# Order of the four products of a quarter tile: both 512-column ones, then both 256-column ones

## The chip, the cores and the metric

The kernel runs on one core of a Trainium2 chip, in one launch. The metric is the device time of that core in microseconds, the median of the runs. Every number below is for this single core.

## The reference, cut to what matters

Two transformer-like blocks run over 256 tokens of width 2048, all in float32. What costs time is the product of the activations with about 400 MB of weights, each weight used once:

```python
# first block: adaptive norm, a wide input projection, a chunked RWKV-7 state, a short convolution
proj = (rms_norm(x, pre_gain) * (1 + scale) + shift) @ w_in     # 2048 x 12416
m = sigmoid(g_a) * ((y_a * silu(z_a)) @ p_a) + sigmoid(g_b) * ((y_b * silu(z_b)) @ p_b)
x = x + gate * rms_norm(m @ w_out, post_gain)                   # 2048 x 2048
# second block: sparse attention (compressed, selected, window), feed-forward, last gate
h = h + nsa_mixer(rms_norm_2(h), ...)                           # w_in 2048 x 5168, w_out 2048 x 2048
h = h + square(relu(rms_norm_2(h) @ ffn_w1)) @ ffn_w2           # 2048 x 8192, 8192 x 2048
h = h + (p @ ple_w_proj) * sigmoid(rms_norm_2(h) @ ple_w_gate)  # 2048 x 2048
```

## The kernel before, in words

**One tile of weights.** Weights come from HBM as a stream of tiles, 128 partitions x 1024 float32 (512 KB), into a ring `raw` of 8. ScalarE copies each tile to `whi` in the type float32r, which TensorE takes in one pass (line 737), VectorE writes the rounding error `raw - whi` to `wlo` (line 1319), both into a ring `wsp` of 4 (`SPLIT`). Activations stand as 512 columns: 256 tokens rounded (the "high" half) and their 256 rounding errors (the "low" half).

**The products.** Weights are the stationary operand, activations the moving one. For one 128 x 128 block of weights TensorE issues two products: `whi` times all 512 columns (line 2197), and `wlo` times the first 256 columns (line 2198). Both accumulate in one PSUM bank; a later step adds the two halves of the bank. Each product is a weight load (LDWEIGHTS) and a matmul, and nothing is shared between two products. A 128 x 1024 tile holds two row blocks `k` (0, 1) by four output blocks `n` (0 to 3). The two row blocks of one `n` are a quarter tile: four products, 512, 256, 512, 256 columns, all into bank `n`. Its last product signals `quarters`, by which ScalarE knows that ring space is free and when a bank is complete.

**`use` (line 2186)** does one tile, or with `part` half of one. In front of a tile it waits for `raw_used` (VectorE has finished the split of this tile, so `whi` and `wlo` are both there), and at the first tile of an output block it waits for `evac_done` (the bank has been read out). `block_of` is eight tiles, the whole depth of 2048. All stages share one TensorE stream written out by hand:

- the opened tiles (`opened_tile`, lines 2246 to 2248), which use three 256-column products per block, then the rest of the first projections (`REST`);
- the `slot(h)` stage: the rest of the input projection, half tiles with the short products of the RWKV-7 chain (`both`, line 2317) between them;
- both output projections of the first block (line 2571, not through `use`), then its `w_out` (tiles `WO0`), the projections of the sparse attention (`NS0`, `QUERY`, `KV0`), its gate columns (lines 2617 and 2618: the same two products with 64 columns of weights) and a compression (line 2632);
- the attention's remaining projections (`NG0`) with attention work between half tiles, then its output projection (`out_tile`);
- the feed-forward part (`ffn`) and the last gate (`PG0`; its last block is three 256-column products, lines 2813 to 2815).

Of the kernel before, what the change touches and what calls it, by code (L numbers as in the profile page):

```python
# [8 lines left out]
P = 128  # L9
T = 256  # L10
D = 2048
KT = D // P
# [276 lines left out]
def block_of_two_layers(nc, stream, vec_in, con_in, x_in, ple_in, lora_in, cmp2_in, out):  # L289
    ctx = ExitStack()  # L290
    with ctx:
# [1891 lines left out]
        def _(pe):  # L2183
            mm = nc.tensor.matmul

            def use(g, i=0, per=RAW, act=None, kt=0, last=KT - 1, bank=0, part=(0, 1, 2, 3), evac=None, off=0):


                n0 = g - WA0
                if part[0] == 0:  # L2190
                    pe.wait_ge(raw_used, i * per + (RAW + in_stream(g) + 1))
                for n in part:
                    if kt == 0 and evac is not None:
                        pe.wait_ge(evac_done, evac[0] + (evac[1] + n + 1))
                    for k in range(2):
                        c = k * 512 + n * P
                        mm(ps[bank + n][:, :], whi[:, n0 % SPLIT, c:c + P], act[:, off + kt + k, :], start=kt + k == 0, stop=False)  # L2197
                        ins = mm(ps[bank + n][:, 0:T], wlo[:, n0 % SPLIT, c:c + P], act[:, off + kt + k, 0:T], start=False,  # L2198
                                 stop=kt + k == last)
                    ins.then_inc(quarters, 1)  # L2200

            def block_of(g0, i, act, evac, per=RAW):

                for j in range(8):
                    use(g0 + j, i, per, act, 2 * j, evac=evac)

            def square_sum(use_, sq_a, sq_t=None, tiles=0):

# [84 lines left out]
            w = OPENED  # L2293
            for r, (blk_, first) in enumerate(REST):
                for j in range(first, 8):
                    use(WA0 + w, act=acts, kt=2 * (j - first), last=KT - 1 - 2 * first, off=2 * first,
                        evac=None if r == 0 else (4 * EARLY + 4 * r - 4, 0))
                    w += 1
            pe.wait_ge(evac_done, 4 * EARLY)
# [8 lines left out]
                        ins.then_inc(quarters, 1)  # L2308
            pe.wait_ge(s.con_loaded, 32)
            def slot(h):  # L2310
                use(WB0 + h // 2, 0, RAW, acts, h // 2 * 2 % KT, part=(0, 1) if h % 2 == 0 else (2, 3),
                    evac=((29 if h >= 16 else 28), h // 16 * 4))

            def both(dst, stationary, moving, start=True, stop=True):
# [259 lines left out]
            E += 32  # L2574
            for j in range(8):
                pe.wait_ge(s.m_done, 2 * j + 2)
                use(WO0 + j, act=acts, kt=2 * j, evac=(E - 4, 0))
            with pe.Fori(1, 4) as b:
                block_of(WO0, b, acts, (b * 4, E - 4))
            E += 16  # L2580
            pe.wait_ge(s.pes_lo, 1)
            for b in range(4):
# [18 lines left out]
            pe.wait_ge(s.pr_out, 6)  # L2601
            for j in range(8):
                pe.wait_ge(s.acts_ready, KT + 2 * j + 2)
                use(NS0 + j, act=acts, kt=2 * j, evac=(E - 4, 0))
                for c in range(2 * j, 2 * j + 2):
                    pe.wait_ge(s.tile_sq, 4 + c + 1)
                    ins = mm(ps[4][:, 0:T], ones, sqx[:, c, :], start=c == 0, stop=c == KT - 1)
            ins.then_inc(s.ss_ps, 1)
            for j in range(8):
                use(NS0 + 8 + j, act=acts, kt=2 * j, evac=(E, 0))  # L2610

            n0 = (GT0 - WA0) % SPLIT
            pe.wait_ge(raw_used, RAW + in_stream(GT0) + 1)
# [27 lines left out]
            for n, kind in enumerate(MIXED):  # L2641
                m = MIXED[:n].count(kind)
                if kind == "C":
                    compress(m)
                else:
                    use(QUERY[m], act=acts, kt=2 * m, evac=(E + 4, 0))
                if n == 8:
                    folded(0)
                if n == 4:
                    pe.wait_ge(s.gt_sig, 1)  # L2650
                    for q in range(2):
                        ins = nc.tensor.transpose(ps[5][:, q * GCOL:(q + 1) * GCOL], gsum[:, q * P:(q + 1) * P], ident[0:GCOL, 0:GCOL])
                    ins.then_inc(s.gt_ps, 1)
            for j in range(8):
                use(KV0 + j, act=acts, kt=2 * j, evac=(E + 8, 0))
                if j == 1:
                    folded(1)
                if j == 5:
                    pe.wait_ge(s.cmp2_in, 16)
                    pe.wait_ge(s.blk_done, 4)  # L2660
                    pe.wait_ge(s.gt_done, 2)
                    mm(ps[4][:, 0:NB], cmp2[:, 0:P], hid[:, 0, :], start=True, stop=True).then_inc(s.cmp_ps, 1)
                    pe.wait_ge(s.hrep_done, GQ)
                    for g in range(GQ):
                        ins = mm(four(5)[:, g, :], hrep[:, g, :], cmp2[:, P:2 * P], start=True, stop=True)
                    ins.then_inc(s.cmp_ps, 1)
# [91 lines left out]

            for g in range(3):
                for k in range(32):  # L2760
                    use(NG0 + 16 * g + k // 2, act=acts, kt=k // 2 * 2 % KT, part=(0, 1) if k % 2 == 0 else (2, 3),
                        evac=(E + 4 * (4 + 2 * g + k // 16) - 4, 0))
                    attention(g, k)
            E += 4 * NG

            def out_tile(j, kt, first, last, e):
                for x in range(2):
                    use(NO0 + j, act=hidn, kt=kt - first, last=last - first, part=(0, 1) if x == 0 else (2, 3), evac=(e - 4, 0),
                        off=first)
                    if j < 12:  # L2770
                        attention(3, 2 * j + x)
# [65 lines left out]
```

## Time and profile before

| | |
|---|---|
| median of 3 runs | 2188.1 us (2186.29 to 2188.31) |
| profiled execution, its own time | 2201.99 us |
| its span, first to last instruction | 2200.3 us |
| TensorE matmul busy | 2163.2 us, 98% |
| TensorE weight loads busy | 1865.9 us, 85% |
| VectorE, ScalarE, GpSimd busy | 71%, 50%, 5% |
| mean DMA rate over the span | 193 GB/s |

The profile gives each matmul a start and a duration, and the durations of neighbours overlap, since matmuls are pipelined. So busy time says little of pace; the distance between two starts does. "Slot" below is the distance from the start of one matmul to the start of the next, "512 slot" that of a 512-column matmul. "PE" is TensorE's matmuls, "PEld" its weight loads, "DVE" VectorE, "ACT" ScalarE.

### The profile page before, as it was taken

How to read it: one execution, taken by the hardware profiler on the slowest of the kernel's cores; microseconds unless marked ns; L12 is line 12 of the kernel's file. 1: busy time of each engine (PE TensorE's matmuls, PEld its weight loads, DVE VectorE, ACT ScalarE, POOL GpSimd, SP SyncE). 2: the span in 40 equal slices, each digit the busy share in tenths (PEclk: the TensorE clock that was granted, in tenths of full speed). 3: DMA queues.
4: the chain of work that ended last, by engine and by line, in shares of the span. 5: the costliest groups of instructions: out<-in, count | busy, mean ns of one | idle time of the engine just before them, and what ended most of it. 6: DMA issues, size and time to landing. Idle time of an engine off the chain costs nothing.

```text
span 2200.3 us, 39494 instructions
## 1 busy us (share of the span) xinstructions
PE 2163.2 (98%) x14640; PEld 1865.9 (85%) x14640; DVE 1571.9 (71%) x2382; ACT 1106.0 (50%) x1749; POOL 109.2 (5%) x96
## 2 busy tenths in 40 slices
PE   8999999999999999999999999999999999999997
PEld 6998887888888888888888878888888888888887
DVE  6985887888887687678666667665575566567767
ACT  3444554555554565465544455444454454445454
POOL 0000000000000100200000002000000000000203
PEclk9999999999999999999999999999999999999999
DMA  9995455455555576566434445556556555555552
GB/s 362 406 377 185 163 182 173 154 173 173 182 164 182 188 252 218 198 199 216 163 126 134 144 153 173 189 183 191 186 167 205 177 192 179 192 189 177 183 181 90
DMA packets 116284, 424.76 MB, mean 193 GB/s; under 512 B 13232, under 2 KB 13616, under 8 KB 115904
## 3 DMA queue, kind: packets, MB, share of 16 engines
q1 hardware_dynamic: 111744, 406.61, 54.9%
q0 software_dynamic: 4416, 16.42, 2.2%
q8 instruction: 88, 1.44, 0.3%
q14 instruction: 36, 0.29, 0.0%
HBM read 414.59 MB, written 8.39 MB: 192 GB/s over the span
## 4 chain that ended last, share of the span: by engine, by line
PE 89%; DVE 7%; ACT 2%; issue 1%; DMA 1%; SPq 0%; DVEq 0%; ACTq 0%
PE ps L2197 46%; PE ps L2198 23%; PE ps L2317 4%; PE ps L2571 2%; DVE wsp L1319 2%; PE ps L2246 2%; PE ps L2247 2%; PE ps L2248 2%; PE ps L2572 1%; ACT wsp L728 1%; PE ps L2729 1%; DVE pr L1978 1%; DMA xt<-in_x 0%; DMA raw<-in_stream 0%; DVE t L1538 0%
## 5 line engine op out<-in xcount | busy, mean ns | idle before, releaser
L2197 PE MATMUL ps<-acts,wsp 128*128 128x512 f32 x3312 | 1201.7, 406 | 4.5 <-DVE stage L1325 1.8
L1319 DVE TENSOR_TENSOR wsp<-raw,wsp 128x1024 fp32r<-128x1024 f32 x629 | 786.9, 1266 | 432.0 <-ACT wsp L728 430.1
L728 ACT ACTIVATE wsp<-raw 128x1024 fp32r<-128x1024 f32 x671 | 703.6, 1058 | 660.3 <-PE ps L2198 578.2
L2198 PE MATMUL ps<-acts,wsp 128*128 128x256 f32 x3312 | 929.9, 281 | 0.0
L2197 PEld LDWEIGHTS ps<-acts,wsp 128*128 128x128 f32 x3312 | 622.3, 188 | 164.2 <-issue 10.1
L2198 PEld LDWEIGHTS ps<-acts,wsp 128*128 128x128 f32 x3312 | 627.0, 189 | 4.3 <-issue 3.3
L2197 PE MATMUL ps<-hidf,wsp 128*128 128x512 f32 x1024 | 362.0, 399 | 0.0
L2198 PE MATMUL ps<-hidf,wsp 128*128 128x256 f32 x1024 | 287.9, 281 | 0.0
L2197 PEld LDWEIGHTS ps<-hidf,wsp 128*128 128x128 f32 x1024 | 192.6, 188 | 48.0
L2198 PEld LDWEIGHTS ps<-hidf,wsp 128*128 128x128 f32 x1024 | 193.9, 189 | 0.0
L728 ACT ACTIVATE half<-ps 128x256 f32<-128x256 f32 (+1 forms) x335 | 125.6, 382 | 64.5 <-PE ps L2198 48.2
L1325 DVE TENSOR_TENSOR s<-ps,half 128x256 f32<-128x256 f32 x160 | 66.2, 423 | 86.5 <-ACT half L728 85.3
L2246 PE MATMUL ps<-acts,wsp 128*128 128x256 f32 x336 | 96.4, 287 | 2.7 <-DVE wsp L1389 2.1
L2247 PE MATMUL ps<-acts,wsp 128*128 128x256 f32 x336 | 95.9, 286 | 0.0
L2248 PE MATMUL ps<-acts,wsp 128*128 128x256 f32 x336 | 95.9, 285 | 0.0
L2197 PE MATMUL ps<-hidn,wsp 128*128 128x512 f32 x256 | 93.0, 405 | 2.0 <-DVE s L1325 1.7
L2571 PE MATMUL ps<-yab,wsp 128*128 128x512 f32 x256 | 90.1, 396 | 0.4 <-DVE wsp L1319 0.4
L1350 DVE SCALAR_TENSOR_TENSOR acc<-raw,cact,acc 128x1024 f32<-128x1024 f32 x57 | 73.1, 1282 | 9.5 <-DMA raw<-in_stream 7.5
L2198 PE MATMUL ps<-hidn,wsp 128*128 128x256 f32 x256 | 72.0, 281 | 0.0
L2572 PE MATMUL ps<-yab,wsp 128*128 128x256 f32 x256 | 71.7, 280 | 0.0
L2246 PEld LDWEIGHTS ps<-acts,wsp 128*128 128x128 f32 x336 | 65.1, 194 | 3.3 <-issue 2.2
L2248 PEld LDWEIGHTS ps<-acts,wsp 128*128 128x128 f32 x336 | 65.1, 194 | 0.0
(343 smaller groups left out, 2143.8 us busy)
## 6 DMA issues: line engine op xcount, KB each, us to landing
raw<-in_stream SPq DMA_DIRECT2D x767, 512.0 KB, 4.2
gate_dram<-stage POOLq DMA_DIRECT2D x32, 128.0 KB, 2.7
gab<-gate_dram POOLq DMA_DIRECT2D x8, 512.0 KB, 5.8
xt<-in_x SPq DMA_DIRECT2D x1, 2048.0 KB, 9.9
xt<-in_x POOLq DMA_DIRECT2D x1, 2048.0 KB, 8.6
ple_dram<-pr__110 POOLq DMA_DIRECT2D x4, 512.0 KB, 3.8
pj<-ple_dram POOLq DMA_DIRECT2D x1, 2048.0 KB, 11.6
out<-y__144 SPq DMA_DIRECT2D x2, 512.0 KB, 2.8
```

What stands on the lines that cost most here:

```text
L728: return nc.scalar.activation(dst, src, ACT.Copy)
L1319: tt(wlo[:, n % SPLIT, :], raw[:, in_stream(g) % RAW, :], whi[:, n % SPLIT, :].bitcast(F32), ALU.subtract).then_inc(raw_used, 1)
L1325: return tt(dst, ps[n if bank is None else bank][:, 0:T], half[:, n % 4, :], ALU.add).then_inc(evac_done, 1)
L1350: stt(dst, raw[:, g % RAW, :], cact[:, j:j + 1], dst, ALU.mult, ALU.add).then_inc(raw_used, 1)
L2197: mm(ps[bank + n][:, :], whi[:, n0 % SPLIT, c:c + P], act[:, off + kt + k, :], start=kt + k == 0, stop=False)
L2198: ins = mm(ps[bank + n][:, 0:T], wlo[:, n0 % SPLIT, c:c + P], act[:, off + kt + k, 0:T], start=False, stop=kt + k == last)
L2246: mm(dst, hi, acts[:, t, 0:T], start=u in STARTS and w % 2 == k == n % 2 == 0, stop=False)
L2247: mm(dst, hi, acts[:, t, T:2 * T], start=False, stop=False)
L2248: ins = mm(dst, lo, acts[:, t, 0:T], start=False, stop=u in ENDS and w % 2 == k == n % 2 == 1)
L2317: ins = mm(dst[lo:hi], stationary[lo:hi], moving[lo:hi], start=start, stop=stop)
L2571: mm(ps[bank][:, :], whi[:, n0 % SPLIT, c:c + P], two(t, x), start=t == 0, stop=False)
L2572: ins = mm(ps[bank][:, 0:T], wlo[:, n0 % SPLIT, c:c + P], yab[:, t, at:at + T], start=False, stop=t == 7)
```

## The change

`use` and `block_of` get an argument `paired`. With it, a quarter tile issues the `whi` products of both row blocks first and then both `wlo` products: 512, 512, 256, 256 columns instead of 512, 256, 512, 256. All four products, their operands, the bank, the waits in front and the signal behind the last are the same. The signal stays on the `wlo` product of the second row block.

```diff
+            def use(..., off=0, paired=False):
                     for k in range(2):
                         c = k * 512 + n * P
                         mm(ps[bank + n][:, :], whi[:, n0 % SPLIT, c:c + P], act[:, off + kt + k, :], start=kt + k == 0, stop=False)
-                        ins = mm(ps[bank + n][:, 0:T], wlo[:, n0 % SPLIT, c:c + P], act[:, off + kt + k, 0:T], start=False,
-                                 stop=kt + k == last)
+                        if not paired:
+                            ins = mm(ps[bank + n][:, 0:T], wlo[...], act[:, off + kt + k, 0:T], start=False, stop=kt + k == last)
+                    if paired:
+                        for k in range(2):
+                            c = k * 512 + n * P
+                            ins = mm(ps[bank + n][:, 0:T], wlo[...], act[:, off + kt + k, 0:T], start=False, stop=kt + k == last)
                     ins.then_inc(quarters, 1)
```

`paired=True` is given in `REST`, `slot`, `WO0` (both its first block and its loop), `NS0`, `QUERY`, `KV0`, `NG0` and `out_tile`. It is not given in `ffn` and in the last gate. Products that don't go through `use` (lines 2246, 2305, 2571, 2594, 2617, 2632, 2813) are untouched.

## Rows read from the trace of the kernel before

**Rows 1.** The profile's page: busy time of each engine, TensorE's granted clock
```profile
PE 2163.2 (98%) x14640; PEld 1865.9 (85%) x14640; DVE 1571.9 (71%) x2382; ACT 1106.0 (50%) x1749; POOL 109.2 (5%) x96
PEclk9999999999999999999999999999999999999999
PE 89%; DVE 7%; ACT 2%; issue 1%; DMA 1%; SPq 0%; DVEq 0%; ACTq 0%
```

**Rows 2.** Groups of instructions: count, busy, mean ns, idle before, releaser
```profile
L2197 PE MATMUL ps<-acts,wsp 128*128 128x512 f32 x3312 | 1201.7, 406 | 4.5 <-DVE stage L1325 1.8
L728 ACT ACTIVATE wsp<-raw 128x1024 fp32r<-128x1024 f32 x671 | 703.6, 1058 | 660.3 <-PE ps L2198 578.2
L2197 PE MATMUL ps<-hidn,wsp 128*128 128x512 f32 x256 | 93.0, 405 | 2.0 <-DVE s L1325 1.7
```

**Rows 3.** Busy time of each engine by stretch: length, then engines, clock, DMA
```profile
155.00:770.00 615.00, 603.35 (x5484) 508.49 (x5483) 473.79 (x786) 315.98 (x529) 23.50 (x46) 1.00 0.54 177
850.00:950.00 100.00, 99.92 (x596) 88.64 (x595) 67.98 (x73) 49.98 (x70) 20.69 (x10) 1.00 0.62 207
1050.00:1300.00 250.00, 247.31 (x1394) 206.15 (x1393) 165.65 (x339) 124.53 (x278) 0.92 (x2) 1.00 0.41 137
1500.00:1900.00 400.00, 400.00 (x2265) 347.14 (x2265) 243.69 (x350) 185.96 (x246) 0.00 (x0) 1.00 0.56 185
```

**Rows 4.** Timeline, `w_out` of the first block: 90 matmuls of line 2197
```profile
859.95 0.39 PE L2197 MATMUL ps<-acts,wsp 128*128 128x512 f32 x1
...
890.80 0.39 PE L2197 MATMUL ps<-acts,wsp 128*128 128x512 f32 x1
```

**Rows 5.** Timeline, feed-forward part: 89 matmuls of line 2197, first three pairs
```profile
1499.83 0.40 PE L2197 MATMUL ps<-hidf,wsp 128*128 128x512 f32 x1
1500.07 0.28 PE L2198 MATMUL ps<-hidf,wsp 128*128 128x256 f32 x1
1500.18 0.40 PE L2197 MATMUL ps<-hidf,wsp 128*128 128x512 f32 x1
1500.41 0.28 PE L2198 MATMUL ps<-hidf,wsp 128*128 128x256 f32 x1
1500.53 0.40 PE L2197 MATMUL ps<-hidf,wsp 128*128 128x512 f32 x1
1500.77 0.28 PE L2198 MATMUL ps<-hidf,wsp 128*128 128x256 f32 x1
1500.89 0.40 PE L2197 MATMUL ps<-hidf,wsp 128*128 128x512 f32 x1
...
1530.92 0.40 PE L2197 MATMUL ps<-hidf,wsp 128*128 128x512 f32 x1
```

**Rows 6.** Timeline, `slot` stage: seven matmuls of line 2197, six pairs
```profile
301.80 0.40 PE L2197 MATMUL ps<-acts,wsp 128*128 128x512 f32 x1
...
303.92 0.40 PE L2197 MATMUL ps<-acts,wsp 128*128 128x512 f32 x1
```

**Rows 7.** Timeline, gate columns (64 columns of weights): nine pairs
```profile
1006.28 0.39 PE L2617 MATMUL ps<-acts,wsp 128*64 128x512 f32 x1
1006.51 0.27 PE L2618 MATMUL ps<-acts,wsp 128*64 128x256 f32 x1
...
1009.34 0.39 PE L2617 MATMUL ps<-acts,wsp 128*64 128x512 f32 x1
```

**Rows 8.** Timeline, last gate's last block: 256-column matmuls only, 23 slots
```profile
2165.22 0.28 PE L2813 MATMUL ps<-acts,wsp 128*128 128x256 f32 x1
...
2167.98 0.28 PE L2815 MATMUL ps<-acts,wsp 128*128 128x256 f32 x1
```

**Rows 9.** The chain of waits: four full float32 matmuls, start and length
```profile
956.13 0.86 PE ps L2607 x4
```

**Rows 10.** Timeline of weight loads in the attention's projections
```profile
957.07 0.19 PEld L2197 LDWEIGHTS ps<-acts,wsp 128*128 128x128 f32 x1
957.18 0.19 PEld L2198 LDWEIGHTS ps<-acts,wsp 128*128 128x128 f32 x1
957.43 0.19 PEld L2197 LDWEIGHTS ps<-acts,wsp 128*128 128x128 f32 x1
```

**Rows 11.** Timeline of matmuls in the same place
```profile
957.18 0.40 PE L2197 MATMUL ps<-acts,wsp 128*128 128x512 f32 x1
957.42 0.28 PE L2198 MATMUL ps<-acts,wsp 128*128 128x256 f32 x1
957.54 0.40 PE L2197 MATMUL ps<-acts,wsp 128*128 128x512 f32 x1
```

More of the change, by code:

```diff
@@ L2184, in _, with use @@
             mm = nc.tensor.matmul
-            def use(g, i=0, per=RAW, act=None, kt=0, last=KT - 1, bank=0, part=(0, 1, 2, 3), evac=None, off=0):
+            def use(g, i=0, per=RAW, act=None, kt=0, last=KT - 1, bank=0, part=(0, 1, 2, 3), evac=None, off=0, paired=False):
                 n0 = g - WA0
@@ L2295, in _ @@
                 for j in range(first, 8):
-                    use(WA0 + w, act=acts, kt=2 * (j - first), last=KT - 1 - 2 * first, off=2 * first,
+                    use(WA0 + w, paired=True, act=acts, kt=2 * (j - first), last=KT - 1 - 2 * first, off=2 * first,
                         evac=None if r == 0 else (4 * EARLY + 4 * r - 4, 0))
@@ L2310, in slot @@
             def slot(h):
-                use(WB0 + h // 2, 0, RAW, acts, h // 2 * 2 % KT, part=(0, 1) if h % 2 == 0 else (2, 3),
+                use(WB0 + h // 2, 0, RAW, acts, h // 2 * 2 % KT, paired=True, part=(0, 1) if h % 2 == 0 else (2, 3),
                     evac=((29 if h >= 16 else 28), h // 16 * 4))
@@ L2576, in _ @@
                 pe.wait_ge(s.m_done, 2 * j + 2)
-                use(WO0 + j, act=acts, kt=2 * j, evac=(E - 4, 0))
+                use(WO0 + j, act=acts, kt=2 * j, evac=(E - 4, 0), paired=True)
             with pe.Fori(1, 4) as b:
-                block_of(WO0, b, acts, (b * 4, E - 4))
+                block_of(WO0, b, acts, (b * 4, E - 4), paired=True)
             E += 16
@@ L2603, in _ @@
                 pe.wait_ge(s.acts_ready, KT + 2 * j + 2)
-                use(NS0 + j, act=acts, kt=2 * j, evac=(E - 4, 0))
+                use(NS0 + j, act=acts, kt=2 * j, evac=(E - 4, 0), paired=True)
                 for c in range(2 * j, 2 * j + 2):
@@ L2609, in _ @@
             for j in range(8):
-                use(NS0 + 8 + j, act=acts, kt=2 * j, evac=(E, 0))
+                use(NS0 + 8 + j, act=acts, kt=2 * j, evac=(E, 0), paired=True)
             n0 = (GT0 - WA0) % SPLIT
@@ L2645, in _ @@
                 else:
-                    use(QUERY[m], act=acts, kt=2 * m, evac=(E + 4, 0))
+                    use(QUERY[m], act=acts, kt=2 * m, evac=(E + 4, 0), paired=True)
                 if n == 8:
@@ L2654, in _ @@
             for j in range(8):
-                use(KV0 + j, act=acts, kt=2 * j, evac=(E + 8, 0))
+                use(KV0 + j, act=acts, kt=2 * j, evac=(E + 8, 0), paired=True)
                 if j == 1:
@@ L2760, in _ @@
                 for k in range(32):
-                    use(NG0 + 16 * g + k // 2, act=acts, kt=k // 2 * 2 % KT, part=(0, 1) if k % 2 == 0 else (2, 3),
+                    use(NG0 + 16 * g + k // 2, paired=True, act=acts, kt=k // 2 * 2 % KT, part=(0, 1) if k % 2 == 0 else (2, 3),
                         evac=(E + 4 * (4 + 2 * g + k // 16) - 4, 0))
@@ L2767, in out_tile @@
                 for x in range(2):
-                    use(NO0 + j, act=hidn, kt=kt - first, last=last - first, part=(0, 1) if x == 0 else (2, 3), evac=(e - 4, 0),
+                    use(NO0 + j, paired=True, act=hidn, kt=kt - first, last=last - first, part=(0, 1) if x == 0 else (2, 3), evac=(e - 4, 0),
                         off=first)
```

8 lines of the change are left out of this document (6 added, 2 removed).

## The prediction

> **What bounds the kernel now.** I read the page first, then the groups of instructions, then stretches, then starts in the timeline. The page shows TensorE matmuls busy 98% of the span, at a clock granted at or near full (2.4 GHz) in all 40 slices, and with 89% of the chain that ended last [rows 1]. The groups show that the idle time right before the 512-column matmuls is 4.5 us in all for those on `acts` and 2.0 us for those on `hidn`, while ScalarE, which makes the high halves, waits 578.2 us for TensorE [rows 2]. So TensorE is the bound and it is hardly ever starved. By stretch this holds in all stages that the change touches: PE is busy 603.35 of 615, 99.92 of 100 and 247.31 of 250 us, VectorE, the next engine, 473.79 of 615, 67.98 of 100 and 165.65 of 250 us [rows 3]. A time that TensorE's stream gains or loses there is therefore a time of the kernel.
>
> Busy time doesn't say at what pace that stream runs; the starts do. In the feed-forward part 89 matmuls of line 2197 start from 1499.83 to 1530.92 us, 88 pairs of a 512 and a 256 slot: 31.09 / 88 = 353.3 ns a pair [rows 5]. The `slot` stage has the same pace, 2.12 / 6 = 353.3 ns [rows 6]. In `w_out` of the first block it is 30.85 / 89 = 346.6 ns [rows 4]: the same instructions, 1.9% faster, for a whole stage. At 2.4 GHz the pair would stream its 768 columns in 320 ns, so 27 to 33 ns of each pair are overhead, and this is all that an order could save or add to.
>
> **Where the overhead sits.** Single slots of the feed-forward part are 0.24, 0.11, 0.23, 0.12, 0.24, 0.12 us (differences of the starts, to 0.01 us) [rows 5]: about 236 for 512 columns and 117 for 256. Stretches of 256-column matmuls alone take 2.76 / 23 = 120 ns a slot [rows 8]. With weights of 64 columns instead of 128 the pair takes 3.06 / 9 = 340.0 ns, the 512 slot 0.23 us [rows 7]. So 340.0 is what streaming costs, about 226.7 + 113.3, and each full-width weight load adds to the slot in which it is done: 353.3 - 340.0 = 13.3 ns for two loads, 6.7 each. The stretch with 256 columns alone agrees: 113.3 + 6.7 = 120.0. A load starts when the matmul before it starts (957.18 and 957.18; 957.43 and 957.42) [rows 10, 11], so one load lies under every matmul, whatever the order. Loads don't end late: the load for a 256-column matmul starts at 957.18, lasts 0.19, and its matmul starts at 957.42.
>
> **The change part by part.** It removes and adds no instruction, wait, transfer or signal. It swaps the second and third product of each quarter tile. Quarter tiles changed: `slot` 128 tiles x 4 = 512; `w_out` 32 tiles, 128; `NS0` 16 tiles, 64; `QUERY` and `KV0` 16 tiles, 64; `NG0` 48 tiles, 192; `out_tile` 32 tiles, 128; `REST` 6 + 6 + 4 + 4 + 2 = 22 tiles, 88. Sum 1176 quarter tiles, 2352 pairs.
>
> Slots of one quarter tile before: 512 to 256, 256 to 512, twice: 2 x 353.3 = 706.7 ns. After: 512 to 512, 512 to 256, 256 to 256, 256 to 512. Three of the four are in the trace: about 236, 120 and 117 ns. The slot from a 512 to a 512 in one pass isn't. From below it is bounded by a matmul that also occupies TensorE for 512 column times, the full float32 one with 256 columns, four in 0.86 us, 215 ns each [rows 9]; nearer is the 512 slot with narrow loads, 227 (340.0 - 113.3) [rows 7]. From above, 240, the longest 512 slot in the timeline [rows 5]. I take 233: 226.7 of streaming plus 6.7 for one load. That is nearest to the same matmul with a full load; if the second 512 is only a shift in when a start is recorded, the same number comes out (236 + 117 - 120 = 233). Sum after: 233 + 236 + 120 + 117 = 706 ns. Change per quarter tile: 0, with ends 215 + 473 = 688 (-19) and 240 + 473 = 713 (+6). On 1176 of them: 0, from -22 to +7 us.
>
> Outside the streams nothing moves. The first product of a quarter still needs only `raw_used`, which covers both halves of the tile. The last product is a 256-column one as before, with the signal on it, so ScalarE's copies and the read-outs of banks see it at the same point of the quarter; what follows it (a product of the chain, an attention product, a 512-column one) is what followed before. SP's queue has its loads gated by `raw_used`, unchanged in place. I cost these at nothing; cover is ScalarE's 660.3 us of idle time in front of its copies [rows 2]. The DMA share of 0.41 to 0.62 in these stretches leaves room if tiles are taken 2% faster [rows 3].
>
> The loads' 6.7 ns deserve a check against a rule. The trace shows a pair of 353.3 ns with loads of 128 columns and 340.0 with loads of 64 [rows 5, 7]. The Trainium skill (TensorE: Matmul & The Clock Gate, "Step-by-step: what each phase is for") says that loading the next weights takes no read bandwidth from the running matmul, since each has its own port, and under "Back-to-back issue gap" it gives N/2.4 + 2.5 ns for a warm matmul, which is 215.8 and 109.2. By the page a quarter tile would take 650 ns in either order, so its change too would be zero. [...]
>
> **The rivals.**
>
> *The fast pace locks in.* The unchanged instruction order runs at two paces, 346.6 and 353.3 ns a pair, each for a whole stage [rows 4, 5]. So the cost of a load isn't fixed: it depends on how loads and streams are phased. A period of four slots may settle at the faster pace where a period of two doesn't. Price: all changed pairs outside `w_out` (2352 - 256 = 2096) gain 6.7 ns: -14.0 us, 2174. For it: the pace exists. Against: nothing ties it to the order; the stages of three 256-column products have a period of three and run at 120 ns, the slow pace.
>
> *Streams of equal length hide the load.* Two 512-column matmuls in a row give the first load no cost: the 512 to 512 slot is 216 to 227. Price: -6 to -17 ns a quarter tile, -7 to -20 us, 2168 to 2181. For it: full float32 matmuls show 215 ns with full-width loads under them [rows 9]. Against: these move half the data per time; the one-pass 512 slot stays at 227 even with narrow loads.
>
> *The phase locks on the slow side, slower than before.* Single pairs of the feed-forward part take 0.36 us (1500.53 to 1500.89) and are made up by the next of 0.35 [rows 5]. If two short slots side by side, each with a full load, leave no room to make it up, each quarter tile carries one step of 6.7 ns more: 1176 x 6.7 = +7.9 us, 2196; if each pair stays at 0.36, +14.0 us outside `w_out` and 256 x 13.4 = +3.4 in it, 2205.5. Place: the two adjacent 256-column slots. It decides from 3.7 ns a quarter tile on (4.4 us in all). For it: 256-column slots alone are never below 120 ns in [rows 8], where alternating ones are about 117; and `w_out` has only pace to lose (256 x 6.7 = 1.7 us). Against: 120 + 233 + 236 + 117 still comes to 706.
>
> *The swap is noticed by nobody* is my forecast itself: each load costs the same under any matmul.
>
> **How the numbers follow.** The sum is made against the profiled execution, 2201.99 us with a span of 2200.3. The runs' median is 13.9 us lower, as a constant that I leave alone. Forecast 2188.1 + 0 = 2188 us, with its own range 2184 to 2192. Less than 0.2% (4.4 us) can't be told from no change here. Chances: no change 0.40; fast pace 0.22 and hidden load 0.14, together 0.36; slow side 0.24. I give the two sides together more than half since the slot that decides isn't in the trace and the pace is known to jump. The range takes in both fast rivals' middles and the first step of the slow one: 2172 to 2197.
>
> **What would show it.** The timeline after should have, in each changed stage, quarter tiles of 706 to 707 ns (starts of every fourth matmul), with slots of about 233, 236, 120 and 117. The feed-forward part must still have 353.3 ns a pair; if it doesn't, its pace depends on how it was entered, and the time moves by up to 1024 x 2 pairs x 6.7 = 13.7 us for a reason that is not the order. A 512 to 512 slot under 229 shows the hidden load; four-slot sums of 693 show the fast pace; of 713 or more, the slow one. `w_out` at 706 instead of 693 would be the 1.7 us loss. Idle time before line 2197 should stay under 10 us; if it grows while slots shrink, the gain was handed to waits for the split. The forecast is wrong if any changed stage has another sum per quarter tile than the two known paces.

## The result, and the profile after

The changed kernel took 2198.11 us (median of 5, 2197.25 to 2199.34), the kernel before 2187.09 us (5, 2186.29 to 2188.31): ratio 1.0046, interval 1.0032 to 1.006, slower by 11 us. I had forecast 2188, no change, in a range to 2197.

The profile after, set beside the one before, doesn't show a slower kernel. Its execution took 2199.34 us (span 2197.6); the one profiled of the kernel before took 2201.99 (span 2200.3). By the two profiles the change gained 2.7 us. Page, busy time:

```profile
PE 2158.0 (98%) x14640; PEld 1871.6 (85%) x14640; DVE 1569.9 (71%) x2382; ACT 1105.8 (50%) x1749; POOL 109.6 (5%) x96
PEclk9999999999999999999999999999999999999999
```

Groups, as in [rows 2] (the 256-column products now have line 2204 where paired, 2199 where not):

```profile
L2197 PE MATMUL ps<-acts,wsp 128*128 128x512 f32 x3312 | 1114.8, 405 | 4.9 <-DVE stage L1325 2.2 <-DVE wt L1325 1.7
L728 ACT ACTIVATE wsp<-raw 128x1024 fp32r<-128x1024 f32 x671 | 703.6, 1058 | 658.3 <-PE ps L2199 325.8 <-PE ps L2204 250.4 <-DMA raw<-in_stream 46.3
L2204 PE MATMUL ps<-acts,wsp 128*128 128x256 f32 x2096 | 413.7, 279 | 0.0
```

TensorE waits no longer (4.9 us against 4.5) and ScalarE as long as before (658.3 against 660.3), so no wait took anything. The pace of the paired products is another than I forecast. Timeline of `w_out` of the first block, the stretch of [rows 4]; each row is now a merged pair of 512-column products, 45 of them, one a quarter tile:

```profile
859.91 0.63 PE L2197 MATMUL ps<-acts,wsp 128*128 128x512 f32 x2
...
890.56 0.62 PE L2197 MATMUL ps<-acts,wsp 128*128 128x512 f32 x2
```

30.65 / 44 = 696.6 ns a quarter tile. My sum said 706. Against the 706.7 of the slow pace this is a gain of 10 ns, against the 693.3 of the fast pace, which [rows 4] had, a loss of 3.3. In the attention's output projection, whose activations lie in a buffer of their own (`hidn`), it is another number. Timeline of its last uninterrupted stretch, first the kernel before (52 products of 512 columns), then the changed one (26 merged pairs):

```profile
1345.78 0.40 PE L2197 MATMUL ps<-hidn,wsp 128*128 128x512 f32 x1
...
1363.80 0.39 PE L2197 MATMUL ps<-hidn,wsp 128*128 128x512 f32 x1
```
```profile
1345.70 0.63 PE L2197 MATMUL ps<-hidn,wsp 128*128 128x512 f32 x2
...
1363.27 0.64 PE L2197 MATMUL ps<-hidn,wsp 128*128 128x512 f32 x2
```

Before 18.02 / 51 = 353.3 ns a pair, 706.7 a quarter tile; after 17.57 / 25 = 702.8. So the paired order doesn't have the same pace in every stage, and the gain is 4 ns here instead of 10. The feed-forward part, untouched, answers to [rows 5] exactly: 89 starts of line 2197, 31.09 / 88 = 353.3 ns a pair.

```profile
1499.65 0.40 PE L2197 MATMUL ps<-hidf,wsp 128*128 128x512 f32 x1
...
1530.74 0.40 PE L2197 MATMUL ps<-hidf,wsp 128*128 128x512 f32 x1
```

A loss of 11 us in the timed executions beside a gain of 2.7 us in the profiles suggests that one of the profiles is not of the kind that was timed. It was the kernel before's: 2201.99 us against a median of 2187 to 2188. The experiments start there.

### The profile page after: what moved, and what is told of

The parts are those of the page before. It is cut to its first block, busy times and chain, and to the rows that moved or that the text cites. A ratio compares the mean times of both kernels' runs of the same rounds, so it can differ in the third digit from the quotient of the medians.

```text
span 2197.6 us, 39494 instructions
## 1 busy us (share of the span) xinstructions
PE 2158.0 (98%) x14640; PEld 1871.6 (85%) x14640; DVE 1569.9 (71%) x2382; ACT 1105.8 (50%) x1749; POOL 109.6 (5%) x96
## 4 chain that ended last, share of the span: by engine, by line
PE 87%; DVE 8%; ACT 2%; issue 2%; DMA 1%; SPq 0%; DVEq 0%; ACTq 0%
PE ps L2197 45%; PE ps L2199 12%; PE ps L2204 10%; PE ps L2323 4%; PE ps L2577 2%; DVE wsp L1319 2%; PE ps L2252 1%; PE ps L2253 1%; PE ps L2254 1%; PE ps L2578 1%; ACT wsp L728 1%; PE ps L2735 1%; DVE acc L1350 1%; DVE pr L1978 1%; DMA xt<-in_x 0%
## 5 line engine op out<-in xcount | busy, mean ns | idle before, releaser
L2197 PE MATMUL ps<-acts,wsp 128*128 128x512 f32 x3312 | 1114.8, 405 | 4.9 <-DVE stage L1325 2.2
L728 ACT ACTIVATE wsp<-raw 128x1024 fp32r<-128x1024 f32 x671 | 703.6, 1058 | 658.3 <-PE ps L2199 325.8
L2197 PEld LDWEIGHTS ps<-acts,wsp 128*128 128x128 f32 x3312 | 551.5, 188 | 81.9 <-issue 13.7
L2204 PEld LDWEIGHTS ps<-acts,wsp 128*128 128x128 f32 x2096 | 393.7, 188 | 93.0
L2204 PE MATMUL ps<-acts,wsp 128*128 128x256 f32 x2096 | 413.7, 279 | 0.0
L2199 PE MATMUL ps<-acts,wsp 128*128 128x256 f32 x1216 | 341.5, 281 | 0.0
L2199 PEld LDWEIGHTS ps<-acts,wsp 128*128 128x128 f32 x1216 | 229.7, 189 | 0.1
L2252 PE MATMUL ps<-acts,wsp 128*128 128x256 f32 x336 | 96.3, 287 | 4.3 <-DVE acts L1362 2.3
L2253 PE MATMUL ps<-acts,wsp 128*128 128x256 f32 x336 | 95.8, 285 | 0.0
L2254 PE MATMUL ps<-acts,wsp 128*128 128x256 f32 x336 | 95.7, 285 | 0.0
L2197 PE MATMUL ps<-hidn,wsp 128*128 128x512 f32 x256 | 82.6, 403 | 2.1 <-DVE s L1325 1.7
L2252 PEld LDWEIGHTS ps<-acts,wsp 128*128 128x128 f32 x336 | 65.2, 194 | 5.1 <-DVE acts L1362 2.9
```

The source lines that it names most:

```text
L728: return nc.scalar.activation(dst, src, ACT.Copy)
L2252: mm(dst, hi, acts[:, t, 0:T], start=u in STARTS and w % 2 == k == n % 2 == 0, stop=False)
L2253: mm(dst, hi, acts[:, t, T:2 * T], start=False, stop=False)
L2254: ins = mm(dst, lo, acts[:, t, 0:T], start=False, stop=u in ENDS and w % 2 == k == n % 2 == 1)
```

## The experiments

### Two levels in the kernel before, and what the paired order does to them

**The kernel before again**, unchanged.

> The kernel before, unchanged, for a second trace. The profile on record took 2201.99 us, 13.9 us more than the timed executions' median, while the changed kernel's profiled execution (2199.34) is one of its timed ones. Theory A (the pace of the feed-forward part jumps): the feed-forward part of the kernel before usually runs at 346.7 ns a pair of products and ran at 353.3 in the profile on record; 2048 pairs x 6.7 = 13.7 us. Then a fast execution's trace (near 2187) has 400 us of it hold about 1154 pairs, not 1133. Rival B (the profiled execution is longer everywhere, and the changed stages are what got slower): the trace near 2187 has 353.3 ns a pair in the feed-forward part and the time is missing elsewhere; a profile of 2202 again would leave it open.

Seven executions at 2185.8 to 2188.8 us, five at 2201.3 to 2204.1; of 35 executions of the same kernel that ran beside it 27 low (to 2190.2) and 8 high (from 2201.0), nothing between. I call these two groups the low and the high level. The profiled one was a high one again (2201.34), so this run shows the two levels but not where they part. Ratio of medians 1.0008, interval 0.9979 to 1.0037.

**Everything in `use` paired.**

```diff
-            def use(..., off=0, paired=False):
+            def use(..., off=0, paired=True):
-            def block_of(g0, i, act, evac, per=RAW, paired=False):
+            def block_of(g0, i, act, evac, per=RAW, paired=True):
```

> The changed kernel, and the paired order in the feed-forward part and the last gate too. In the changed kernel's trace a quarter tile in paired order takes about 691 and 702 ns in turn, mean 696.5 (348.3 a pair). Theory A: the feed-forward part in paired order takes 348.3 ns a pair instead of the 353.3 it has in the changed kernel: 2048 + 256 pairs x 5 = 11 us faster than the changed kernel, about 2187, the same as before within 3 us. Rival B (paired order is what costs time): 1024 more quarter tiles at the same loss as the 1176 changed ones, +9 us, about 2207.

2187.31 us, all 12 executions between 2186.14 and 2188.96; 0.998 of before (0.996 to 1.0). Theory A's number was met, and with 1120 more quarter tiles paired (2048 pairs in the feed-forward part and 192 in the last gate, where the expectation counted 256) the time fell by 11 us against the first measurement of the changed kernel, where rival B wanted 9 us more. There was one level only.

**The feed-forward part paired alone**, from the kernel before.

```diff
-                    block_of(FF0, f * 8 + b, acts, (f * 32 + b * 4, E - 4))
+                    block_of(FF0, f * 8 + b, acts, (f * 32 + b * 4, E - 4), paired=True)
   # and the same for both uses of FF0 + 32
```

> The kernel before with the paired order in the feed-forward part alone (its eight first tiles and all other stages keep the old order). Theory A: if the usual pace of the old order there is 346.7, paired order at 348.3 costs 2048 x 1.6 = +3 us: 2190; the stages ahead stay as before. Rival B: +9 us, 2196.

2192.02 us (2190.53 to 2194.02), one level; 0.9995 (0.9972 to 1.0017). 2 us over theory A's number, 4 below B's. It goes with the run above: with the feed-forward part paired there is no high level. Theory A had the stages ahead stay as before, and in this run's trace (an execution of 2194.02 us, its longest) one did not. `w_out` of the first block, whose order is the old one here as in [rows 4], 86 products of 512 columns:

```profile
860.74 0.40 PE L2197 MATMUL ps<-acts,wsp 128*128 128x512 f32 x1
...
890.78 0.40 PE L2197 MATMUL ps<-acts,wsp 128*128 128x512 f32 x1
```

30.04 / 85 = 353.4 ns a pair, against 346.6 in [rows 4]. So the old order jumps between its two paces in this stage too; on its 256 pairs that is 1.7 us. Whether this makes up the 2 us of the median isn't shown, since only one execution has a trace.

**The last stage ahead in the old order**, from the changed kernel, and **that stage paired alone**, from the kernel before; both were run twice.

```diff
-                    use(NO0 + j, paired=True, act=hidn, ...)     # from the changed kernel
+                    use(NO0 + j, act=hidn, ...)
```

> The changed kernel with the old order in the attention's output projection, the last stage ahead of the feed-forward part; everything else as changed. Theory A with the pace set by how the feed-forward part is entered: the entry is as in the kernel before, so the fast pace may come back: 2198 - 13.7 = 2184. Rival B: the cost is spread over all changed stages, 128 of 1176 quarter tiles are undone: -1 us, 2197. Rival C: the entry is set by a stage further ahead or by chance: 2198 or mixed runs of 2184 and 2198.

> The kernel before with the paired order in the attention's output projection alone, the last stage ahead of the feed-forward part: the mirror of the run that took it away. The kernel before had two levels, 2186 to 2190 and 2201 to 2204 (35 executions, 8 high); so had the changed kernel without this edit (2184 and 2197, 4 of 12 high), while the changed kernel had five executions at 2197 to 2199. Theory A (this edit fixes the entry to the feed-forward part on the slow pace): all or nearly all executions high, near 2201. Rival C (the share of high executions is chance, five of five too): two levels again, about a quarter high. Rival B (a cost per quarter tile): one level near 2189.

The first: 8 executions at 2182.6 to 2184.3, 4 at 2196.9 to 2197.6. The second: 4 at 2185.4 to 2187.9 and 8 at 2201.1 to 2204.7, beside 3 high of 23 for the kernel before. That looked like the entry deciding the pace, so I ran the changed kernel again.

> The changed kernel again, for the spread of its executions. Theory A: all 12 near 2198. Rival C: two levels, 2184 and 2198, with most at 2184.

Seven at 2183.0 to 2184.6, five at 2196.9 to 2198.4. So the changed kernel has both levels as well, and my first five executions had all been on its high one. "Fixes the entry" fell with this. Whether the share of high ones moves stayed open until the repeats:

> The changed kernel again, for the share of its executions on the high level: 5 of 5 and 5 of 12 so far, the kernel before 16 of 92. Theory H (the paired order in the last stage ahead makes the slow pace of the feed-forward part more likely): clearly more than a fifth, 5 to 9 of 12. Theory C (the share is the same as before's and the first five were chance): 1 to 4 of 12.

> The changed kernel with the old order in the attention's output projection, again: 4 of 12 high so far. Theory H: the share of the kernel before, 1 to 4 of 12. If it is as high as the changed kernel's, the cause lies in another changed stage than the last.

> The kernel before with the paired order in the attention's output projection alone, again: 8 of 12 high so far. Theory H: 5 or more of 12. Theory C: 1 to 4 of 12.

High executions were 4, 8 and 4 of 12, and of the kernel before beside them 16 of 29. Both repeats turned the earlier order round (4 then 8 of 12; 8 then 4 of 12), and the kernel before went from 3 of 23 to 16 of 29 with no line changed. These two groups ran on different chips (0 and 13 in the record; the others on 12, 1, 2 and 9), so the chip is one candidate for the share; no chip had two groups, and that of the first measurement isn't on record. Side by side on one chip the changed kernel had 5 of 12 against 3 of 23, then 4 of 12 against 16 of 29. Theory H isn't supported: the share varies more from one group of runs to the next than between these kernels. Over all timed runs:

| kernel | executions | low level, median | high level, median | high | mean |
|---|---|---|---|---|---|
| before | 155 | 2187.3 | 2202.1 | 41 | 2191.4 |
| changed | 29 | 2184.0 | 2198.2 | 14 | 2190.7 |
| everything in `use` paired | 23 | 2187.1 | none | 0 | 2187.2 |
| all stages paired (below) | 11 | 2186.6 | none | 0 | 2186.8 |

Level by level the changed kernel is 3.4 and 3.9 us faster (0.15% and 0.18%). On one chip side by side the low levels lie 3.0 us (chip 0) and 3.2 us (chip 13) apart.

**Where the levels part.** The profiles of this last group of runs fell on the low level. Stretch 1500 to 1900 us, instructions in it: first the changed kernel's high execution (2199.34 us), then its low one of the third measurement (2184.36 us):

```profile
1500.00:1900.00 400.00, 400.00 (x2267) 1.00 0.56 186
```
```profile
1500.00:1900.00 400.00, 400.00 (x2310) 1.00 0.59 189
```

In the same 400 us the feed-forward part issues 43 products more. The low execution's timeline, 90 starts of line 2197:

```profile
1499.86 0.39 PE L2197 MATMUL ps<-hidf,wsp 128*128 128x512 f32 x1
...
1530.71 0.39 PE L2197 MATMUL ps<-hidf,wsp 128*128 128x512 f32 x1
```

30.85 / 89 = 346.6 ns a pair, against 353.3 in the high one. The kernel before itself left no trace on the low level. The nearest to it is that kernel with the attention's output projection alone paired, which left one on each level, 2203.26 us and, in the repeat, 2186.5 us. The same 400 us, high, then low:

```profile
1500.00:1900.00 400.00, 400.00 (x2266) 1.00 0.58 185
```
```profile
1500.00:1900.00 400.00, 400.00 (x2310) 1.00 0.59 189
```

Two marks bracket the difference in the changed kernel: the gate columns' last product and the last block's first one (columns: count, duration min/median/max, first and last start). High execution, then low:

```profile
L2623 PE MATMUL ps<-acts,wsp x16: 388/388/389, 1003.7 to 1008.8; 128*64 128x512 f32 x16
L2819 PE MATMUL ps<-acts,wsp x64: 283/283/388, 2160.8 to 2183.6; 128*128 128x256 f32 x64
```
```profile
L2623 PE MATMUL ps<-acts,wsp x16: 388/388/388, 1003.6 to 1008.7; 128*64 128x512 f32 x16
L2819 PE MATMUL ps<-acts,wsp x64: 279/283/387, 2145.8 to 2168.6; 128*128 128x256 f32 x64
```

Between them 1152.0 us and 1137.1 us, 14.9 of the 15.0 us between the two executions. Up to 1008.7 they are alike, and so they are up to the last product of the attention's output projection (1364.6 and 1364.5). The rest of the stretch is the feed-forward part and the last gate, whose old-order products follow it. High execution (72 products), then low (73):

```profile
2114.85 0.40 PE L2197 MATMUL ps<-acts,wsp 128*128 128x512 f32 x1
...
2139.93 0.40 PE L2197 MATMUL ps<-acts,wsp 128*128 128x512 f32 x1
```
```profile
2114.93 0.39 PE L2197 MATMUL ps<-acts,wsp 128*128 128x512 f32 x1
...
2139.89 0.39 PE L2197 MATMUL ps<-acts,wsp 128*128 128x512 f32 x1
```

25.08 / 71 = 353.2 ns and 24.96 / 72 = 346.7 ns. With 2048 pairs in the feed-forward part and 192 in the last gate, 2240 x 6.7 = 15.0 us: one pace from the entry to the end accounts for the whole distance of the levels.

Where it is set shows in one trace, the repeat of the changed kernel with the old order in the attention's output projection (2184.55 us, low). The feed-forward part begins there at 1366 us; at 1382 to 1384 us ten products for a sum of squares stand between its tiles. Ahead of them 28 products of 512 columns, behind them 29:

```profile
1366.28 0.40 PE L2197 MATMUL ps<-acts,wsp 128*128 128x512 f32 x1
...
1375.82 0.40 PE L2197 MATMUL ps<-acts,wsp 128*128 128x512 f32 x1
```
```profile
1385.02 0.40 PE L2197 MATMUL ps<-acts,wsp 128*128 128x512 f32 x1
...
1394.72 0.40 PE L2197 MATMUL ps<-acts,wsp 128*128 128x512 f32 x1
```

9.54 / 27 = 353.3 ns, then 9.70 / 28 = 346.4. So this break can change the pace. The same break in the last gate, near 2094 us on the low level and 2107 on the high one, changed it in none of the 12 traces of kernels that keep the old order there.

### What sets the pace

**A fixed entry to the feed-forward part.** At its eighth tile TensorE waits for its own first quarter and issues a spare product of 80 or 72 columns; on the changed kernel, and with 80 on the kernel before.

```diff
                 for n in part:
+                    if lead and n == 1:
+                        pe.wait_ge(quarters, 4 * (SPLIT + g - WA0) + 1)
+                        mm(ps[7][:, 0:lead], acts[:, 0, 0:P], acts[:, 0, 0:lead], start=True, stop=True)
```

> The changed kernel with a fixed entry to the feed-forward part: at its eighth tile TensorE waits for its own first quarter tile and then issues one spare product of 80 columns into a free bank. By themselves, stretches in the old order behind such a product took 346.7 ns a pair, quiet and with traffic. Cost of the wait and product: about 0.5 us. Theory A (the pace is set by the phase in which the two streams of loads and products start, and then holds): one level near 2184.5, no execution near 2198, the trace with 346.7 ns a pair through the feed-forward part. Rival E (the pace is set anew by each wait or by what other engines do): two levels again.

> The same with 72 columns, behind which the old order took 353.5 ns a pair. Theory A: one level near 2198.5, 14 us above the 80-column one, though the spare product is 8 columns (3 ns) shorter. Rival E: the same spread as with 80 columns.

> The kernel before with the 80-column entry, to compare the two orders at one pace of the feed-forward part. Theory A: one level near 2187.5, so the changed kernel is 3 us faster (0.15%) where the feed-forward part runs alike. Rival B (the paired order costs time in the changed stages): at or below the changed kernel with the same entry.

High were 10, 11 and 10 of 12 (medians 2198.6, 2199.18 and 2201.53), while 5 of 29 of the kernel before, on the same chip, were. 80 and 72 columns did the same, and the expectation of one low level failed. The two widths are no test of the phase, though: in both traces of the changed kernel the next product starts 132 to 134 ns behind the spare one, so the narrower one shifted nothing. What the runs do show is that the entry matters: the kernel before was high in 10 of 12 behind this stop and in 5 of 29 without it. The 80-column pair keeps the order of the kernels: high level 2198.7 against 2201.9.

**The orders by themselves.** This and the next two kernels leave the whole computation out.

```python
pe.wait_ge(go, ...)                                  # an idle gap
mm(ps[6][:, 0:pad], w, acts[:, 0, 0:pad])            # the leading product
for w, n: four products in one of the orders         # 48 in all
```

> A kernel that leaves the whole computation out (it writes zeros) and holds 48 stretches of 48 products each, on weights and activations that lie still: four orders (512 and 256 in turn; paired; 512 alone; 256 alone), each behind an idle gap and one leading product of 64, 72, 80, 88, 96 or 104 columns, which shifts where the stretch starts by 3.3 ns a step; the first 24 stretches with TensorE alone, the other 24 with VectorE and ScalarE at work on 1024-column tiles. Theory A (two paces from the phase alone): the order in turn takes 346.7 or 353.3 ns a pair, by the leading product; paired takes 691 to 707 a quarter tile; 256 alone 117.5 or 120 a product; a 512 to 512 slot about 233. Rival D (the two paces come from the traffic of VectorE, ScalarE and the transfers): one pace for every leading product in the first half, another in the second. My forecast's sum (233 + 236 + 120 + 117 = 706) would show as 706 whatever the leading product.

Two stretches in turn (512, 256) behind 72 and 80 columns, first and last of 24 starts of the 512-column line:

```profile
37.61 0.48 PE L100 MATMUL ps<-acts,wsp 128*128 128x512 f32 x1
...
45.81 0.40 PE L100 MATMUL ps<-acts,wsp 128*128 128x512 f32 x1
...
46.68 0.47 PE L100 MATMUL ps<-acts,wsp 128*128 128x512 f32 x1
...
54.74 0.40 PE L100 MATMUL ps<-acts,wsp 128*128 128x512 f32 x1
```

8.20 against 8.06 us for the same 23 pairs: 6.1 ns a pair. From the 5th start to the 45th the old order takes 346.6 to 346.7 ns in 5 stretches and 352.9 to 353.6 in 7, with 3 of 6 slow in the quiet half and 4 of 6 under traffic: rival D falls, since both paces came with TensorE alone. The paired order takes 696.6 to 697.3 ns a quarter tile in all 12, 512 alone 226.7 to 227.3 a slot, 256 alone 119.7 to 120.0. Paired and 256 alone, first group of each (a merged row has x2):

```profile
83.43 0.63 PE L100 MATMUL ps<-acts,wsp 128*128 128x512 f32 x2
83.90 0.39 PE L104 MATMUL ps<-acts,wsp 128*128 128x256 f32 x2
84.13 0.62 PE L100 MATMUL ps<-acts,wsp 128*128 128x512 f32 x2
...
136.39 11.14 PE L125 MATMUL ps<-acts,wsp 128*128 128x512 f32 x48
...
205.33 6.00 PE L129 MATMUL ps<-acts,wsp 128*128 128x256 f32 x48
```

The slots in the paired order repeat as 233, 236, 116, 113 and 232, 231, 113, 119 ns: 698 and 695. A 512 slot is 227 where only such slots stand, 231 to 236 here. The slow pace of the old order has a pattern of three pairs, 232, 118, 240, 120, 236, 114 ns (behind 72 columns), 1060 in all; the fast one is 230, 117 over and over behind 64, and a longer pattern with the same mean behind 80.

The leading product did not do what I built it for. Behind 72 and behind 80 columns:

```profile
37.48 0.30 PE L109 MATMUL ps<-acts,wsp 128*128 128x72 f32 x1 [0.21 <-POOL gpt L88]
46.55 0.30 PE L109 MATMUL ps<-acts,wsp 128*128 128x80 f32 x1 [0.21 <-POOL gpt L88]
```

The stretches start at 37.61 and 46.68, both 0.13 us later. In this and the next two kernels the distance is 132 or 133 ns for 64, 72, 80 and 88 columns, 149 or 150 for 96 and 152 or 153 for 104. So there were three distances and not six, and no steps of 3.3 ns.

**More entries, and longer groups.**

```python
order "four":  L L L L  S S S S      order "eight": 8 L, then 8 S      (L 512, S 256 columns)
```

> A second kernel of stretches alone (it leaves the whole computation out and writes zeros), quiet, 48 products each. The old order 36 times: leading products of 64 to 104 columns, each three times behind GpSimd's answer and three times behind TensorE's own last product. Then three orders behind leading products of 64 to 88 columns: paired, four (both 512-column products of two output blocks, then their four 256-column ones) and eight (all eight 512-column products of a tile, then all eight 256-column ones). The spare product of 80 and of 72 columns in the feed-forward part gave mostly the slow pace, both of them (10 and 11 of 12). Theory A1 (the phase of the start decides, and 8 columns shift it): each width has its own pace, three times of three. Theory A2 (the start has a phase against something that the program does not control): the same width gives both paces among its repeats. For the orders: paired 696.7 ns per four products whatever the start; from 226.7 for a 512 to 512 slot and 120 for a 256 to 256 one, four comes to 693 and eight to 1387 per eight products (346.7 a pair) if the changes from 512 to 256 and back cost nothing more.

The old order was slow in 3 of 18 stretches behind GpSimd's answer and in 0 of 18 behind TensorE's own product; 72, 80 and 104 columns each gave both paces. A1 falls as far as one width was to have one pace, and A2 holds; that 8 columns shift the start wasn't tested, as they didn't. Paired took 348.3 to 348.4 ns a pair in 8 of 8, four 350.8 to 350.9, eight 348.9 to 349.2. Neither beat pairing, and both lie above the 346.7 that the slots of unmixed streams add up to. A fixed cost for each change between long and short doesn't explain it, since the fast pace of the old order changes at every product and takes just 346.7.

**Waits and signals in the stream.**

```diff
+                    if order in ("waits", "both"):
+                        pe.wait_ge(filled, KT + 8)
+                        if order in ("signals", "both") and not (l and n == 3):
+                            ins.then_inc(quart, 1)
```

> A third kernel of stretches alone (no computation, zeros written), all in the old order, 96 products each, 12 stretches of each of four kinds: no wait and no signal inside; a wait in front of each weight tile on a semaphore long reached; a signal behind each quarter tile; both, as in the feed-forward part. Theory F (waits or signals inside the stream push it to the slow pace, which is why the feed-forward part behind a spare product was slow in 31 of 36 executions while quiet stretches behind one were slow in 3 of 36): stretches with waits or signals are mostly at 353.3 ns a pair, those without at 346.7. Theory G (they don't; only how the stretch starts counts): the same small share of slow stretches in all four kinds.

Behind GpSimd's answer 4, 2, 2 and 2 of 6 stretches were slow (none, waits, signals, both); behind TensorE's own product all 24, in each of the four kinds. So waits and signals inside are not needed for the slow pace, as theory G has it; its small share of slow stretches did not come. But the same entry, TensorE's own product, was never slow in the run before and always in this one, which is another program (96 products a stretch instead of 48) on another chip (13 instead of 2). Inside this run the starts repeat themselves: behind GpSimd's answer, with waits alone or signals alone, the stretches behind 80 columns were slow 4 of 4 times, those behind 64 and 72 never in 8. Two stretches without waits, both behind 64 columns, 48 starts each, the first behind GpSimd's answer, the second behind TensorE's own product:

```profile
82.13 0.48 PE L86 MATMUL ps<-acts,wsp 128*128 128x512 f32 x1
...
98.52 0.39 PE L86 MATMUL ps<-acts,wsp 128*128 128x512 f32 x1
...
134.00 0.48 PE L86 MATMUL ps<-acts,wsp 128*128 128x512 f32 x1
...
150.69 0.40 PE L86 MATMUL ps<-acts,wsp 128*128 128x512 f32 x1
```

16.39 and 16.69 us. Each stretch keeps its pace from its fifth start to its end.

### A version without the high level

From the all-paired kernel, also the two output projections of the first block (the edit shown) and, in the same way, the short projection ahead of `slot`:

```diff
                             mm(ps[bank][:, :], whi[...], two(t, x), start=t == 0, stop=False)
+                        for k in range(2):
+                            c, t = k * 512 + n * P, 2 * j % 8 + k
                             ins = mm(ps[bank][:, 0:T], wlo[...], yab[:, t, at:at + T], start=False, stop=t == 7)
```

> All stages paired as in the run with the feed-forward part and the last gate paired, and also the two output projections of the first block and the short decay and gate projection, which have loops of their own (256 + 16 pairs in the old order till now). The paired order has shown one pace, 348.3 ns a pair, at every start; the old order 346.7 or 353.3. Expected: one level, 12 of 12 within 3 us, at 2187.3 - 272 x 5 ns x the share that ran slow = 2186 to 2187. Below the kernel before's mean of its two levels (2189 to 2195 by session) and the changed kernel's (2189 to 2190), above their low levels (2184 for the changed kernel). If two levels show up here too, the paired order isn't immune.

> The run with everything in use paired, once more in another session: so far 12 of 12 between 2186.1 and 2189.0. If the paired order is immune: one level at 2187.3 again, whatever share of the kernel before's executions is high alongside. If its single level was chance: a second level near 2190 to 2200.

2186.6 us (11 executions, 2186.05 to 2188.36), 0.9981 of before (0.9961 to 1.0001); the repeat of everything in `use` paired 2187.13 (11, 2185.99 to 2189.36), 0.9997 (0.9988 to 1.0006). Both have one level, while 4 of 21 executions of the kernel before beside them were high. As a mean of all executions the kernel with all stages paired is 4.6 us below the kernel before (3.7 on the chip that both ran on) and 3.9 below the changed one. Against their low levels it is 0.7 us faster and 2.6 us slower, so it beats the changed kernel only on average and in its worst case.

## Why the prediction was wrong, point by point

**"As a constant that I leave alone."** This is the step that failed. The profiled execution was 13.9 us over the median of the same kernel, and I called that a constant of profiling. The runs showed the feed-forward part and the last gate at 353.3 instead of 346.6 ns: 2048 + 192 pairs x 6.7 = 15.0 us, where the levels lie 14.8 us apart. The two numbers stood in my text, the 13.9 in the sum and 13.7 (for the feed-forward part alone) in the last paragraph as what the time would move by if that pace changed, and I did not put them together. The median that I forecast from was of executions on the low level, the rows that I summed of one on the high level. The 2198.11 us that I missed is the changed kernel's high level: all five of its executions were on it and all five of the kernel before on the low one. By the share of its later runs (9 of 24) five high ones in a row come less than once in a hundred times, so chance alone is a poor account of that part, and what else it was stays open. On its low level, 2184.0 us, it would have lain in my range, by luck and not by a right sum. The profiles of the changed kernel show no such constant: 2199.34 us is inside its own timed range.

**"Outside the streams nothing moves."** Right as to waits: TensorE's idle time before line 2197 was 4.9 us against 4.5. The feed-forward rows of the two profiles are alike only because both executions were on the high level.

**"Each full-width weight load adds to the slot in which it is done."** The pace was read rightly, the split was wrong. With full-width loads under every product, 512 alone takes 226.7 a slot, and the 512 slots with narrow loads, which I had split off in proportion, are 226 to 228 ns in the trace [rows 7]: there the full load costs nothing. A cost per load can't be added up; it depends on what stands beside it.

**"233 + 236 + 120 + 117 = 706."** Measured 696.6. The slot that I had to guess, 512 to 512, was near (233 and 232), and 512 to 256 too (236 and 231). The one that I took from a row of its own kind, 256 to 256, missed: 116 and 113 here, 120 in a stream of its own kind. The term's size was off by 9 ns a quarter tile, inside its bounds (688 to 713), and by 3 in the attention's output projection. It is also not all of the effect: -10 ns on the 920 quarter tiles on `acts` outside `w_out`, -4 on the 128 on `hidn` and +3.3 on the 128 of `w_out` would be -9.3 us, and the levels moved by -3.4 and -3.9. In the two profiles the part from the last opened tile to the output projections of the first block (600 changed quarter tiles) went from 587.8 to 585.7 us, so it gained 2.1 us and not 6. The sum takes every pair as part of an unbroken stretch at the slow pace, and between half tiles there the short products of the chain stand; how much of the rest each of these took isn't shown. I had 0, with my own range from -4 to +4.

**The rivals.** "The fast pace locks in" has its core confirmed, two paces of one order, but not as a result of pairing: the paired order has a pace of its own, 1.7 ns a pair above the fast one (4.7 in the attention's output projection), and it is the old order, left in the feed-forward part, that jumps. "Equal lengths hide the load" is true of 512 alone and not of two in a row. "The phase locks on the slow side" put it at the two short slots; they were the quick ones. None of the three had the rival that came about: that the untouched stages are at either pace from one execution to the next. My last paragraph had it as a sign to look for, without a chance.

**What stays open.** Every execution of the changed kernel in the first measurement was high, 5 of 5, and 9 of 24 later. I can't show that the change has no part in the share; the repeats show that it varies from one group of runs to the next (3 of 23 and 16 of 29 for one kernel), and that a stop ahead of the feed-forward part raises it (31 of 36). What sets the pace at a start is not found. Both paces come without traffic and without waits or signals inside, and one width of the leading product gives both. The distance of the start from the leading product took three values only, so a phase at the start is neither shown nor ruled out, and neither is the chip. Nor is it shown why the paired order is slower on `hidn`: in kernel.py this buffer starts 32 bytes off a multiple of 64 and `hidf` (696.7 in the all-paired kernels) on one, which no run varied.

## What to carry to other kernels

When the profiled execution lies apart from the timed ones, find the stage in which before using either; here 0.6% was the last 2240 pairs of the stream at another pace, not the profiler. List single executions, not only a median: two levels 14 us apart make medians of five say +0.46% for a change that is worth -0.15% at the same level. And in a stream of products bound by TensorE, prefer the order that showed no second pace at its entries (512, 512, 256, 256 here) when the other order's two paces lie on both sides of it, and measure it on each buffer that it reads.

## What the runs showed of the hardware

One-pass 512 and 256-column products in turn, a full weight load under each, have two steady paces, 346.7 and 353.3 ns a pair, at the same granted clock (1.00 in both stretches, the 2.4 GHz level). The slow one repeats every three pairs. A stretch kept its pace to its end, for 17 us by itself and, in the kernel's traces, from the break in the first block of the feed-forward part to the last gate's old-order products, some 750 us, through all waits between. The order 512, 512, 256, 256 showed no second pace at any entry: 696.7 ns in 19 of 20 stretches by themselves (697.3 in the other), and the two kernels without the old order in the feed-forward part and the last gate had one level in 34 of 34 executions. But its pace differed by buffer, 696.6 ns on `acts` and 702.8 on `hidn`, in the same kernel. 512-column slots alone are 226.7 ns (227.3 at most), 13 ns over the 213.3 that 512 columns take at 2.4 GHz, and neither the work of VectorE and ScalarE nor 64 instead of 128 columns of weights made them shorter; 256-column slots alone are 120.

The Trainium skill (TensorE: Matmul & The Clock Gate, "Back-to-back issue gap") gives N/2.4 + 2.5 ns for a warm matmul, 215.8 and 109.2 by it, and says itself that this is the gap of a single matmul and not of a stream with weight loads. It has no term for the order. The full float32 products of 256 columns took 215 ns each [rows 9], the one-pass ones of 512 columns 226.7, and here the measurement decides.
